# Two-model block on one core: seven-product blocks in another order, the norm scale at the residual, and a further seven-product block in quarter 0

## The chip, the cores and the metric

One NeuronCore of one Trainium2 chip runs the whole program. The metric is the device time of one execution in microseconds (us). The kernel is written against the engines directly: each engine (TensorE = PE, VectorE = DVE, ScalarE = ACT, GpSimd = POOL, SyncE = SP) has its own instruction list, and counting semaphores order them. Each engine works through its own list strictly in order.

## The reference, cut to what matters

512 tokens of width 1024 pass through a recurrent mixer, an attention mixer and then two identical hybrid layers. Only the feed-forward part at the end of each hybrid layer is touched here:

```python
def rmsnorm(x, g):
    xf = x.astype(jnp.float32)
    xf = xf * lax.rsqrt(jnp.mean(xf * xf, axis=-1, keepdims=True) + EPS)
    return (xf * g.astype(jnp.float32)).astype(x.dtype)
...
    x = x + merged @ w_o
    h2 = rmsnorm(x, norm_mlp)
    return x + jnp.square(jax.nn.relu(h2 @ w_up)) @ w_down
```

D_FF is 4096, so `w_up` is 1024 x 4096 and `w_down` 4096 x 1024. The norm's per-token factor s = 1/rms is positive, so relu(s a)^2 = s^2 relu(a)^2: the factor may be applied to the products of `w_up`, or squared and applied to the products of `w_down`.

## The kernel before

Everything is kept transposed: a tile is 128 features by 512 tokens. A **turn** (or block) gives 512 output features by 512 tokens in a set of four PSUM banks; the two sets of four banks alternate from turn to turn. Operands are split into a high and a low part of a short float format, so every product is three matmuls (high x high, low x high, high x low; L741, L742, L743). The weights come in **chunks** of 128 x 1024 numbers: SP loads a chunk into one of four `w_raw` slots, ACT rounds it into `w_hi` (L1132, `round_ahead`), and DVE subtracts to get `w_lo` (L1582, `remainder`). `w_hi` and `w_lo` have four slots as well, so a chunk can be prepared once PE has finished the chunk four places before it, and three chunks are normally ready ahead.

The feed-forward part works by **quarters** of D_FF. A quarter has two up blocks (j = 0, 1), each giving 512 features in `up_t` and then in `y_hi`/`y_lo` (relu, square, split), and two down blocks (kind `residual`, k = "y"), which multiply all 1024 features of the quarter with `w_down` and add the result to `x`. A plain block is 4 chunks of 24 matmuls over 512 tokens.

In quarters 1 to 3 both up blocks are **seven-product blocks**: a block multiplication of 2 x 2 parts that needs seven products in place of eight (`seven_products`, L753). Each product is a chunk of 24 matmuls over 256 tokens (L781, L783, L785). Four loaded weight quarters are combined on DVE (L1578, L1587, L1590, L1593, in place in `w_raw`) to four further chunks: B11, T1, T2, B21, T3, B22, T4 is the order. The combined inputs `mixed` are made once per layer in quarter 0 by the step `mix` (part 0 gives the first mixed input, part 1 the low parts of the other three). Partial sums that go to several outputs are copied by ACT, the **seeds** (L1159): after product 1 the bank `first` is copied into the bank `sum_`, after product 2 `lent` into `kept_t`, after product 3 `sum_` into `last`, after product 5 `sum_` into `kept_t`. PE's product 3 (T2) accumulates into `sum_` and so waits for the first seed.

What sets the order of work is the step list of `schedule()` and, for each step, the order in which each engine's function writes its instructions: on ACT `split_ahead` (weights and seeds of the block), then `join` (a wait for all that the engines did before), then the step's own work; on DVE the same without seeds. `led` says that a block's chunk 3 was prepared by the step before. In `up_of_seven` DVE waits for the end of the block, then reads all four banks, scales by `rms`, squares and splits, and ACT makes the high parts in between.

## Time and profile before

| what | value |
|---|---|
| median of 3 runs | 2188.85 us (2188.39 to 2189.55) |
| the profiled execution's own time | 2187.33 us |
| its span (first to last instruction) | 2185.5 us |
| PE busy | 2123.3 us, 97% of the span |
| DVE busy | 1429.0 us, 65% |
| ACT busy | 906.1 us, 41% |
| DMA | 212.02 MB, the queue that carries the weights takes 31.0% of 16 engines' time |
| mean granted PE clock | 0.988 |

The page says how much of the span each engine is busy, which wait was the longest, and how the chain of work that ended last divides: here 78% of it is PE. Matmuls overlap in the pipeline (each is shown 0.38 us long and starts 0.216 us after the one before), so their rate is read from start times.

### The profile page before, as it was taken

Reading aid. Unit: us, or ns where it says so; the run is one execution under the profiler, and the core shown is the slowest. Engines: PE = TensorE matmul, PEld = TensorE weight load, DVE = VectorE, ACT = ScalarE, POOL = GpSimd, SP = SyncE. Lnnn points to the kernel's source line nnn. Section 1 sums busy time; section 2 is a strip of 40 time slices with the busy share of each in tenths; the row PEclk is TensorE's granted clock in tenths of the full one; section 3 lists DMA queues with packets and bytes.
Section 4 is the critical chain, followed back from the end, with each engine's and each line's share of the span. In section 5 each row is a group of like instructions: output and inputs, shape, how many; then the busy total and the mean of one; then the engine's idle time right before and its main releaser. Section 6 shows DMA issues by size and latency. Waiting matters only on the chain.

```text
span 2185.5 us, 27736 instructions
## 1 busy us (share of the span) xinstructions
PE 2123.3 (97%) x11076; PEld 1871.5 (86%) x11086; DVE 1429.0 (65%) x1984; ACT 906.1 (41%) x1271; POOL 1.4 (0%) x6
## 2 busy tenths in 40 slices
PE   9989999999999999999988989999999999989888
PEld 8878878788888888888888988888888888889887
DVE  8888785768665554566677576665445656776665
ACT  6775473636344213234333244443212224342342
POOL 0000000000000000000000000000000000000000
PEclk9999999999999999999999999999999999999999
DMA  5333212223332323333231333233333333232322
GB/s 180 114 100 103 87 59 86 70 82 97 97 96 78 106 87 116 106 89 106 86 114 51 116 116 106 78 92 91 98 105 98 105 101 89 81 116 77 116 93 91
DMA packets 59535, 212.02 MB, mean 97 GB/s; under 512 B 6736, under 2 KB 7120, under 8 KB 59280
## 3 DMA queue, kind: packets, MB, share of 16 engines
q1 hardware_dynamic: 59040, 208.83, 31.0%
q8 instruction: 88, 1.44, 0.3%
q0 software_dynamic: 224, 1.31, 0.2%
q14 instruction: 39, 0.32, 0.0%
q10 hardware_dynamic: 144, 0.12, 0.0%
HBM read 208.14 MB, written 2.10 MB: 96 GB/s over the span
## 4 chain that ended last, share of the span: by engine, by line
PE 78%; DVE 8%; ACT 2%; issue 1%; DVEq 0%; ACTq 0%
PE bank L741 20%; PE bank L742 20%; PE bank L743 20%; PE bank L781 2%; PE bank L783 2%; PE bank L785 2%; PE bank L736 2%; PE bank L737 2%; PE bank L738 2%; DVE w_lo L1582 1%; PE bank L973 1%; DVE arena L2269 1%; ACT w_hi L1132 1%; PE bank L965 1%; DVE y_lo L1636 0%
## 5 line engine op out<-in xcount | busy, mean ns | idle before, releaser
L1582 DVE TENSOR_TENSOR w_lo<-w_raw,w_hi 128x1024 fp32r<-128x1024 f32 x423 | 508.4, 1214 | 580.5 <-ACT w_hi L1132 579.2
L1132 ACT ACTIVATE w_hi<-w_raw 128x1024 fp32r<-128x1024 f32 x423 | 436.6, 1046 | 727.4 <-PE bank L743 641.7
L741 PE MATMUL bank<-h_both,w_hi 128*128 128x512 f32 x1404 | 535.8, 382 | 2.1 <-DVE arena L1631 1.1
L742 PE MATMUL bank<-h_both,w_hi 128*128 128x512 f32 x1404 | 532.1, 379 | 0.0
L743 PE MATMUL bank<-h_both,w_lo 128*128 128x512 f32 x1404 | 532.1, 379 | 0.0
L741 PE MATMUL bank<-y_hi,w_hi 128*128 128x512 f32 x1048 | 399.0, 381 | 7.8 <-DVE y_lo L1636 5.8
L742 PE MATMUL bank<-y_lo,w_hi 128*128 128x512 f32 x1048 | 397.8, 380 | 0.0
L743 PE MATMUL bank<-y_hi,w_lo 128*128 128x512 f32 x1048 | 397.8, 380 | 0.0
L741 PEld LDWEIGHTS bank<-h_both,w_hi 128*128 128x128 f32 x1404 | 265.4, 189 | 42.8 <-issue 3.9
L742 PEld LDWEIGHTS bank<-h_both,w_hi 128*128 128x128 f32 x1404 | 265.4, 189 | 38.4 <-issue 1.4
L743 PEld LDWEIGHTS bank<-h_both,w_lo 128*128 128x128 f32 x1404 | 265.4, 189 | 37.8
L741 PEld LDWEIGHTS bank<-y_hi,w_hi 128*128 128x128 f32 x1048 | 198.4, 189 | 38.0 <-DVE w_lo L1582 4.5
L743 PEld LDWEIGHTS bank<-y_hi,w_lo 128*128 128x128 f32 x1048 | 198.5, 189 | 28.3
L742 PEld LDWEIGHTS bank<-y_lo,w_hi 128*128 128x128 f32 x1048 | 198.5, 189 | 28.1 <-issue 0.2
L1197 ACT ACTIVATE y_hi<-arena 128x512 fp32r<-128x512 f32 x144 | 86.9, 630 | 187.7 <-DVE arena L2269 69.8
L781 PE MATMUL bank<-mixed,w_hi 128*128 128x256 f32 x384 | 112.4, 293 | 36.9 <-DVE y_lo L1636 36.9
L781 PEld LDWEIGHTS bank<-mixed,w_hi 128*128 128x128 f32 x384 | 79.3, 206 | 37.9 <-issue 37.9
L783 PE MATMUL bank<-mixed,w_hi 128*128 128x256 f32 x384 | 111.4, 290 | 0.0
L785 PE MATMUL bank<-mixed,w_lo 128*128 128x256 f32 x384 | 111.0, 289 | 0.0
L1631 DVE TENSOR_TENSOR arena<-bank,rms 128x512 f32<-128x512 f32 x120 | 76.0, 686 | 22.8 <-PE bank L743 21.7
L1636 DVE TENSOR_TENSOR y_lo<-arena,y_hi 128x512 fp32r<-128x512 f32 x128 | 79.7, 683 | 0.2 <-ACT y_hi L1197 0.2
L781 PE MATMUL bank<-h_both,w_hi 128*128 128x256 f32 x288 | 79.6, 276 | 0.0
(271 smaller groups left out, 2492.9 us busy)
## 6 DMA issues: line engine op xcount, KB each, us to landing
w_raw<-in_stream SPq DMA_DIRECT2D x389, 512.0 KB, 3.7
x<-in_x_t SPq DMA_DIRECT2D x8, 256.0 KB, 6.9
out_t<-x SPq DMA_DIRECT2D x8, 256.0 KB, 2.1
arena<-in_consts POOLq DMA_DIRECT2D x1, 1024.0 KB, 5.3
w_raw<-in_stream SPq DMA_DIRECT2D x2, 256.0 KB, 4.3
arena<-in_positions POOLq DMA_DIRECT2D x1, 256.0 KB, 6.0
vec_t<-in_vecs ACTq DMA_DIRECT2D x1, 112.5 KB, 3.3
ident<-in_consts SPq DMA_DIRECT2D x1, 64.0 KB, 6.9
```

Source lines behind the costliest of these rows:

```text
L736: pe.matmul(out, a_h[:, t], w_h, start=first, stop=False)
L741: pe.matmul(out, w_hi[:, slot, w], streamed(a_h), start=first, stop=False)
L742: pe.matmul(out, w_hi[:, slot, w], streamed(a_l), start=False, stop=False)
L743: mm = pe.matmul(out, w_lo[:, slot, w], streamed(a_h), start=False, stop=last)
L781: pe.matmul(out, w_hi[:, slot, w], tokens(tile(0, k)), start=begin, stop=False, skip_group_check=True)
L783: pe.matmul(out, w_hi[:, slot, w], tokens(tile(1, k)), start=False, stop=False, skip_group_check=True)
L785: mm = pe.matmul(out, w_lo[:, slot, w], tokens(tile(0, k)), start=False, stop=end, skip_group_check=True)
L1132: A.activation(w_hi[:, slot, w], w_raw[:, chunks.raw_slot[raw], w], ACT.Copy).then_inc(hi_ready, 1)
L1197: A.activation(y_hi[:, slot, :], src, ACT.Copy).then_inc(a_hi, 1)
L1582: V.tensor_tensor(w_lo[:, slot, w], src[:, w], w_hi[:, slot, w].bitcast(F32), ALU.subtract).then_inc(lo_ready, 1)
L1631: V.tensor_tensor(halves(tile(n)), product_bank(n), halves(rms[:, :]), ALU.mult).then_inc(evacuated, 1)
L1636: V.tensor_tensor(y_lo[:, slot(n), :], tile(n), y_hi[:, slot(n), :].bitcast(F32), ALU.subtract).then_inc(a_lo, 1)
```

## The change

1. `first_up` runs `mix` part 0, up block j = 0 (plain), `mix` part 1, and then up block j = 1 as a seven-product block. Before it ran up 0, `mix` 0, up 1, `mix` 1, with both blocks plain.
2. The norm's factor is no longer applied to the up products. The statistics are taken in quarter 0's first down block, ACT writes the mean of squares without the root (Identity in place of Sqrt), and DVE multiplies each down product by its reciprocal before it is added to `x` (`scaled_residual`): two DVE operations per bank in place of one.
3. Seven-product blocks have an order of their own on ACT and DVE (`seven`). ACT reads `first` after product 4 and `sum_` after the block's end (Relu), squares two tiles, and the squares and high parts of these two tiles (`left_over`) are moved behind the first seed of the next block if that is a seven-product block too. DVE reads only `last` and the kept tiles, and multiplies with relu in one operation.
4. The plain up block has relu, square and high part on ACT, and only the low part on DVE.
5. The tiles of `y` are made and used in the order 2, 3, 0, 1 (`PART_ORDER`), and the rows of `w_down` are laid out to suit.

```diff
     "merge": {"vec": 4, **SPLIT},
-    "up": {"vec": 4, **SPLIT},
+    "up": {"act_out": 4, **SPLIT},
...
-        return [s("up", 4, 1, True, j=0), s("mix", part=0), s("up", 4, 1, j=1, led=True), s("mix", part=1)]
-
-    def down():
-        return [s("residual", 4, 1, k="y", j=0), s("residual", 4, 1, k="y", j=1)]
+        return [s("mix", part=0), s("up", 4, 1, j=0, led=True), s("mix", part=1), s("up", 0, 1, j=1, seven=True)]
+
+    def down(stats=False):
+        return [s("residual", 4, 1, stats, k="y", j=0, scaled=True), s("residual", 4, 1, k="y", j=1, scaled=True)]
```

On ACT, the new function `seven`:

```diff
+                if not step.args.get("led"):
+                    act.wait_ge(bank_ready, before)
+                    ahead(3)
+                products(1)
+                keep(sum_, first)
+                run_left_over()
+                ahead(4)
+                products(2)
+                keep(kept(T, 0), lent)
+                ahead(5)
+                products(3)
+                keep(last, sum_)
+                ahead(6)
+                products(4)
+
+                act.wait_ge(a_lo, T.value("a_lo"))
+                act.wait_ge(evacuated, before)
+                positive(first, slice(0, SEQ // 2)).then_inc(evacuated, 1)
+                ahead(7)
+                products(5)
+                keep(kept(T, 1), sum_)
+                ahead(8)
+                products(6)
+                ahead(9)
+                for n in (2, 3):
+                    act.wait_ge(vec, T.value("vec", n + 1))
+                    hi(n, up_t[:, n, :], slot + n)
+                act.wait_ge(bank_ready, done)
+                positive(sum_, slice(SEQ // 2, SEQ)).then_inc(evacuated, 3)
+                ahead(10)
...
+                left_over.append(rest)
+                if not step.args["paired"]:
+                    run_left_over()
...
-                A.activation(rms[:, :], bank[set_ + 3][:, :], ACT.Sqrt, scale=1.0 / D,
+                squared = step.kind == "residual"
+                A.activation(rms[:, :], bank[set_ + 3][:, :], ACT.Identity if squared else ACT.Sqrt, scale=1.0 / D,
```

On DVE, in `scaled_residual` (the order of a down block is scale 0, scale 1, add 0, scale 2, add 1, scale 3, add 2, add 3; at the program's last block it is scale and add, bank by bank):

```diff
+                def scale(n):
+                    nonlocal counted
+                    banks(n)
+                    V.tensor_tensor(halves(up_t[:, n, :]), product_bank(n), halves(rms[:, :]), ALU.mult).then_inc(vec, 1)
...
+                def add(n):
+                    got(scaled_at[n])
+                    x_n = x[:, 4 * j + n, :]
+                    V.tensor_tensor(x_n, up_t[:, n, :], x_n, ALU.add).then_inc(evacuated, 1)
```

And on DVE, its `seven`:

```diff
+                ahead(4)
+                run_left_over()
+                for n in range(5, 9):
+                    ahead(n)
...
+                V.tensor_tensor(up_pair(2, slice(SEQ // 2, SEQ)), kept_sum, kept_lent, ALU.add).then_inc(vec, 1)
+                ahead(9)
+                dve.wait_ge(chunk_used, T.value("used", 6))
+                V.tensor_tensor(up_pair(2, slice(0, SEQ // 2)), last, kept_lent, ALU.add).then_inc(vec, 1)
+                got(2)
+                for n in range(2, 4):
                     V.scalar_tensor_tensor(out=up_t[:, n, :], in0=up_t[:, n, :], scalar=0.0, in1=up_t[:, n, :],
                                            op0=ALU.max, op1=ALU.mult).then_inc(vec, 1)
+                low(2, 1)
+                low(3, 2)
+                ahead(10)
```

**Place one: ACT, from the end of a pair's first seven-product block into its second (quarters 1 to 3).** `w_hi` is a chunk's high part, `y_hi<-arena` the high part of an up tile, `bank<-bank` the first seed, on which product 3 of the second block waits. Before:

```order
L1132 ACTIVATE w_hi<-w_raw 128x1024 x3
L1197 ACTIVATE y_hi<-arena 128x512 x4
L1159 ACTIVATE bank<-bank 128x512
L1132 ACTIVATE w_hi<-w_raw 128x1024
L1159 ACTIVATE kept_t<-bank 128x512
```

Now:

```order
L1192 ACTIVATE arena<-bank 128x2x256
L1154 ACTIVATE w_hi<-w_raw 128x1024
L1189 ACTIVATE kept_t<-bank 128x512
L1154 ACTIVATE w_hi<-w_raw 128x1024 x2
L1274 ACTIVATE y_hi<-arena 128x512 x2
L1192 ACTIVATE arena<-bank 128x2x256
L1154 ACTIVATE w_hi<-w_raw 128x1024
L1189 ACTIVATE bank<-bank 128x512
L1229 ACTIVATE arena<-arena 128x512 x2
L1274 ACTIVATE y_hi<-arena 128x512 x2
L1154 ACTIVATE w_hi<-w_raw 128x1024
```

Four high parts stood ahead of the first seed; now two high parts, a relu read of a bank and one chunk stand there, and two squares and two high parts stand behind it.

**Place two: DVE, in quarter 0, around the second mixing (before, the first mixing and up block 1 stand with it).** `arena<-x,vec_t,arena` are the mixing sums, `mixed` their low parts. Before:

```order
L1582 TENSOR_TENSOR w_lo<-w_raw,w_hi 128x1024
L2226 SCALAR_TENSOR_TENSOR arena<-x,vec_t,arena 128x256 x4
L2234 SCALAR_TENSOR_TENSOR arena<-x,vec_t,arena 128x256 x4
L2243 TENSOR_TENSOR mixed<-arena,mixed 128x1024
L1582 TENSOR_TENSOR w_lo<-w_raw,w_hi 128x1024 x3
L1631 TENSOR_TENSOR arena<-bank,rms 128x512 x4
L2294 SCALAR_TENSOR_TENSOR arena<-arena 128x512 x4
L1636 TENSOR_TENSOR y_lo<-arena,y_hi 128x512 x4
L2229 SCALAR_TENSOR_TENSOR arena<-x,vec_t,arena 128x256 x4
L2237 SCALAR_TENSOR_TENSOR arena<-x,vec_t,arena 128x256 x4
L2243 TENSOR_TENSOR mixed<-arena,mixed 128x1024 x3
L1582 TENSOR_TENSOR w_lo<-w_raw,w_hi 128x1024 x4
```

Now:

```order
L1667 TENSOR_TENSOR w_lo<-w_raw,w_hi 128x1024
L1675 TENSOR_TENSOR w_raw<-w_raw 128x1024
L1667 TENSOR_TENSOR w_lo<-w_raw,w_hi 128x1024
L2416 TENSOR_TENSOR y_lo<-arena,y_hi 128x512 x4
L2350 SCALAR_TENSOR_TENSOR arena<-x,vec_t,arena 128x256 x4
L2358 SCALAR_TENSOR_TENSOR arena<-x,vec_t,arena 128x256 x4
L2364 TENSOR_TENSOR mixed<-arena,mixed 128x1024 x3
L1667 TENSOR_TENSOR w_lo<-w_raw,w_hi 128x1024
L1678 TENSOR_TENSOR w_raw<-w_raw 128x1024
L1667 TENSOR_TENSOR w_lo<-w_raw,w_hi 128x1024 x5
```

Before, two down blocks followed the second mixing; now the seven-product block j = 1, whose product 3 reads the first of these three `mixed` low parts, is the very next block. The scale and the squares (L1631, L2294) have left DVE for ACT.

## Rows read from the trace of the kernel before

**Rows 1.** The page's busy time, share and instructions of each engine.

```profile
PE 2123.3 (97%) x11076; PEld 1871.5 (86%) x11086; DVE 1429.0 (65%) x1984; ACT 906.1 (41%) x1271; POOL 1.4 (0%) x6
```

**Rows 2.** The waits, PE's two largest: us in total, times, longest us.

```profile
PE bank L781 <- DVE y_lo L1636: 36.9, 6, 6.2
...
PE bank L741 <- DVE y_lo L1636: 5.8, 3, 3.4
```

**Rows 3.** Six stretches, one per seven-product pair: sum in us, busy times and means.

```profile
sum 276.41, PE 239.51 PEld 238.54 DVE 193.59 ACT 125.79 POOL 0.00; mean PE 39.92 PEld 39.76 DVE 32.26 ACT 20.97 POOL 0.00
```

**Rows 4.** PE in order of time: first matmuls of blocks, and after the stall.

```profile
995.57 0.38 PE L741 MATMUL bank<-h_both,w_hi 128*128 128x512 f32 x1
...
1080.78 0.27 PE L781 MATMUL bank<-h_both,w_hi 128*128 128x256 f32 x1
...
1099.53 0.28 PE L781 MATMUL bank<-h_both,w_hi 128*128 128x256 f32 x1
...
1111.21 0.55 PE L781 MATMUL bank<-mixed,w_hi 128*128 128x256 f32 x1 [6.15 <-DVE y_lo L1636]
...
1126.76 0.38 PE L741 MATMUL bank<-y_hi,w_hi 128*128 128x512 f32 x1
...
1168.20 0.27 PE L781 MATMUL bank<-h_both,w_hi 128*128 128x256 f32 x1
```

**Rows 5.** ACT in order of time, before the second block's first seed.

```profile
1109.34 1.23 ACT L1197 ACTIVATE y_hi<-arena 128x512 fp32r<-128x512 f32 x2 [1.23 <-DVE arena L2269]
1110.48 0.58 ACT L1159 ACTIVATE bank<-bank 128x512 f32<-128x512 f32 x1
```

**Rows 6.** Stretches with a PE pause: the third figure from the end is the granted clock.

```profile
1104.98:1111.20 6.22, 0.08 (x1) 0.03 (x1) 6.19 (x10) 3.09 (x6) 0.00 (x0) 0.80 0.00 0
1111.20:1116.04 4.84, 4.83 (x25) 4.84 (x26) 3.48 (x4) 2.26 (x3) 0.00 (x0) 0.55 0.30 78
284.00:290.00 6.00, 4.27 (x20) 3.44 (x19) 5.84 (x9) 2.72 (x4) 0.00 (x0) 1.00 0.07 10
```

**Rows 7.** PE in quarter 0: the second down chunk waits for `y_lo`.

```profile
1041.82 0.48 PE L741 MATMUL bank<-y_hi,w_hi 128*128 128x512 f32 x1 [1.20 <-DVE y_lo L1636]
```

**Rows 8.** DVE and ACT in a pair's first block (it starts at 1168.20).

```profile
1166.56 2.54 DVE L1829 TENSOR_TENSOR x<-bank,x 128x512 f32<-128x512 f32 x4 [1.02 <-PE bank L743]
...
1179.12 1.06 ACT L1132 ACTIVATE w_hi<-w_raw 128x1024 fp32r<-128x1024 f32 x1 [1.14 <-PE bank L785]
...
1185.26 1.23 DVE L1590 TENSOR_TENSOR w_raw<-w_raw 128x1024 f32<-128x1024 f32 x1
```

**Rows 9.** Groups of instructions by line and shape: busy us, mean ns, idle before.

```profile
L1636 DVE TENSOR_TENSOR y_lo<-arena,y_hi 128x512 fp32r<-128x512 f32 x128 | 79.7, 683 | 0.2 <-ACT y_hi L1197 0.2
L1281 ACT ACTIVATE arena<-x 128x512 f32<-128x512 f32 x44 | 27.0, 622 | 18.1 <-DVE x L1829 12.3 <-DVE sumsq L1746 4.4 <-DVE sumsq L1743 1.0
L2263 DVE TENSOR_TENSOR arena<-bank,kept_t 128x512 f32<-128x512 f32 x12 | 9.2, 770 | 0.0
```

**Rows 10.** ACT and DVE in quarter 0: after the norm, up block 1, second mixing.

```profile
1000.94 1.99 ACT L1132 ACTIVATE w_hi<-w_raw 128x1024 fp32r<-128x1024 f32 x2
...
1036.23 2.54 DVE L1631 TENSOR_TENSOR arena<-bank,rms 128x512 f32<-128x512 f32 x4 [0.89 <-PE bank L743]
...
1041.09 2.49 DVE L1636 TENSOR_TENSOR y_lo<-arena,y_hi 128x512 fp32r<-128x512 f32 x4
1043.77 1.67 DVE L2229 SCALAR_TENSOR_TENSOR arena<-x,vec_t,arena 128x256 f32<-128x256 f32 x4 [0.20 <-issue]
...
1047.06 3.50 DVE L2243 TENSOR_TENSOR mixed<-arena,mixed 128x1024 fp32r<-128x1024 f32 x3
...
1048.03 2.94 ACT L1132 ACTIVATE w_hi<-w_raw 128x1024 fp32r<-128x1024 f32 x3
```

**Rows 11.** DVE at the end of the program.

```profile
2169.60 1.28 DVE L1829 TENSOR_TENSOR x<-bank,x 128x512 f32<-128x512 f32 x2
...
2172.87 0.68 DVE L1829 TENSOR_TENSOR x<-bank,x 128x512 f32<-128x512 f32 x1
```

More of the change, by code:

```diff
@@ L293, in schedule @@
             after.args["led"] = True
+            step.args["paired"] = bool(after.args.get("seven"))
     return items
@@ L1137, in split_ahead @@
                     part_before[0] = step.args.get("part")
-                if step.args.get("seven") and step.args.get("led"):
-                    seeds(0)
                 for n, slot in [next_slot(T)] if runs_ahead(step) else split_slots(T, step):
@@ L1147, in split_ahead, with run_left_over, seven, products @@
                     round_ahead(n, slot)
-                    if step.args.get("seven"):
-                        seeds(n - RING + 1)
-            def seeds(used):
+            left_over = []
+            def run_left_over():
+                while left_over:
+                    left_over.pop(0)()
+            def seven(step):
+                part_before[0] = None
                 set_ = 4 * (T.fixed["turn"] % 2)
                 first, lent, sum_, last = (bank[set_ + n][:, :] for n in range(4))
-                for at, out, src in ((1, sum_, first), (2, kept(T, 0), lent), (3, last, sum_), (5, kept(T, 1), sum_)):
-                    if at == used + 1:
-                        act.wait_ge(chunk_used, T.value("used", at))
-                        A.activation(out, src, ACT.Copy).then_inc(seeded, 1)
+                slot = 4 * step.args["j"]
+                before, done = T.value("turn", 0, 4), T.value("turn", 4, 4)
+                def products(n):
+                    act.wait_ge(chunk_used, T.value("used", n))
+                def ahead(n):
+                    round_ahead(n, (T.fixed["chunk"] + n) % RING)
+                def keep(out, src):
+                    A.activation(out, src, ACT.Copy).then_inc(seeded, 1)
+                def positive(src, t):
+                    return A.activation(up_pair(0, t), bank_pair(src), ACT.Relu)
+                if not step.args.get("led"):
[27 more added lines that the diff above has]
+                ahead(10)
+                outs = T.value("act_out")
+                def rest():
+                    for n in range(2):
+                        act.wait_ge(evacuated, done)
+                        A.activation(up_t[:, n, :], up_t[:, n, :], ACT.Square).then_inc(act_out, 1)
+                    for n in range(2):
+                        act.wait_ge(act_out, outs + n + 1)
+                        hi(n, up_t[:, n, :], slot + n)
+                left_over.append(rest)
+                if not step.args["paired"]:
+                    run_left_over()
@@ new lines, in _, with run_left_over, seven, ahead @@
+            left_over = []
+            def run_left_over():
+                while left_over:
+                    left_over.pop(0)()
+            def seven(step):
+                last = bank_pair(the_bank(3)[:, :])
+                kept_lent, kept_sum = (bank_pair(kept(T, n)) for n in range(2))
+                slot, highs = 4 * step.args["j"], T.value("a_hi")
+                def ahead(n):
+                    remainder(n, (T.fixed["chunk"] + n) % RING)
+                def low(n, count):
+                    dve.wait_ge(a_hi, highs + count)
+                    V.tensor_tensor(y_lo[:, slot + n, :], up_t[:, n, :], y_hi[:, slot + n, :].bitcast(F32),
+                                    ALU.subtract).then_inc(a_lo, 1)
+                if not step.args.get("led"):
+                    ahead(3)
+                ahead(4)
+                run_left_over()
+                for n in range(5, 9):
+                    ahead(n)
+                dve.wait_ge(a_lo, T.value("a_lo"))
+                dve.wait_ge(evacuated, T.value("turn", 0, 4))
+                dve.wait_ge(seeded, T.value("seeds", 4))
+                V.tensor_tensor(up_pair(2, slice(SEQ // 2, SEQ)), kept_sum, kept_lent, ALU.add).then_inc(vec, 1)
[4 more added lines that the diff above has]
+                for n in range(2, 4):
@@ L2309, in emit @@
             def emit(step):
+                if step.args.get("seven"):
+                    seven(step)
+                    return
                 closing = step.args.get("part") == "close" and step.kind in ("x", "lru_gate", "residual")
@@ L2370, in order_of_weights @@
             q = args["quarter"]
-            out.append(group(w_down[layer], [(512 * j, 512)], slice(1024 * q, 1024 * q + 1024)))
+            rows = np.concatenate([np.arange(P) + 1024 * q + P * k for k in Y_ORDER])
+            out.append(group(w_down[layer], [(512 * j, 512)], rows))
         elif kind == "forget":
```

123 lines of the change are left out of this document (69 added, 54 removed).

## Prediction, made before the changed kernel had run

> **What bounds the kernel now.** The page comes first: PE is busy for 2123.3 of 2185.5 us [rows 1], so only two things can pay: less matmul work, and the some 62 us in which PE waits. The view of waits says where they are: 36.9 us in six pauses at L781, the longest 6.2, and 5.8 us at L741 [rows 2]. The stretches then give the price of the six. A pair of seven-product blocks should take two blocks' work. The first block of the pair at 1080.78 lasts 18.75 us, to 1099.53 [rows 4]; its second, to 1126.76, lasts 27.23. The six pairs took 276.41 us [rows 3] where 12 x 18.76 = 225.1 is work, so the pauses cost **51.3 us**, 8.55 each, and not 6.15. The rest is the clock: it was granted at 0.80 on average over the pause and at 0.55 in the 4.84 us after it [rows 6], so most of the product behind the pause ran at the lower level, 1.2 GHz.
>
> Who is late? PE's product 3 adds into a bank that ACT seeds, and that seed (L1159) starts at 1110.48, ends at 1111.06, and PE starts at 1111.21 [rows 4, 5]. DVE's `y_lo`, which the view names, merely ended near that time. The seed's source was ready long before; ACT stood in its list at the previous block's high parts, which wait for DVE's squares [rows 5]. An earlier seed is therefore worth the whole 51.3.
>
> **The change, part by part.** *The pairs lose the old pause*: -51.3. *Two blocks (one per layer) have seven products in place of eight*: a plain block takes (1168.20 - 1126.76)/2 = 20.72 us [rows 4], a seven-product block 18.75, so 2 x 1.97 = -3.9. *Quarter 0's down block waited for `y_lo`*: the pause shown is 1.20, and 1.36 from start to start (a matmul is drawn 0.38 long at a rate of 0.216); block j = 1 is now finished tile by tile as in the other quarters, so 2 x 1.36 = -2.7 [rows 7].
>
> *New wait in the pairs.* I count from the first block's start (1168.20 in rows 8). The second block starts at 18.75, and its product 3 is due two products of 2.68 later, at 24.1. ACT used to round chunk 7 at 10.92; now the relu read of `first` stands ahead, a bank read of 0.58 that holds ACT for about 0.55 [rows 5]. DVE's chain of splits and combinations, which waits for this chunk and ended at 1186.49, i.e. at 18.3 [rows 8], ends at 18.85. Behind it, in each engine's order: ACT rounds T2, to 20.0 (1.06); DVE splits it, to 21.2 (1.23); it adds the bank `last`, to 21.9 (0.77 [rows 9], with the usual overlap of 0.1); two squares, to 23.2; ACT makes the second high part, to 23.9; relu read of `sum_`, to 24.4; ACT rounds chunk 10, to 25.35; only then the seed, to 25.85; PE starts 0.15 later, at **26.0**. That is 1.9 late, six times: **+11.4**. The wait DVE has from doubled work at the down block (eight operations at 0.6 from -1.64 on, to 3.25 where it was 0.9 [rows 8]) is covered: chunk 3 is split by 4.4 and needed at 8.0. In the second block the seed for product 5 is done some 0.1 ahead of its use, so a little more may be lost there. The lower bound of the new wait is nothing (a chain of twelve steps has to be 1.9 shorter), the upper 3.5 (each step 0.13 longer).
>
> Does such a pause lower the clock? The gaps of 1.7 us near 287 show none: granted 1.00 [rows 6]. The pause of 6.15 does. 1.9 is much nearer to 1.7 than to 6.15, so I take no clock loss; the price of one, 2.25 a pair, stays in the range.
>
> *New wait in quarter 0.* The new seven-product block follows up block 0 at once, and its product 3 needs the second mixing and a seed. Count from up block 0's start at 995.57 [rows 4]. It ends at 20.7, and product 3 is due at 20.7 + 5.4 = 26.1. Ahead of the relus stand the first mixing and three chunks with their combinations. From the norm's end on ACT, 5.4 in (1000.94 [rows 10]): chunk 3 and four small copies until the first sum at 7.7; eight sums, 3.3 [rows 10]; a high part, 1.06; chunk 4, 0.95; its split and two combinations, 3.85; T1's split and the third combination, 2.4; T2's rounding, 1.1 [rows 8]. ACT comes to the relus at 20.35, where the banks would allow 19.1 (1.64 ahead of the block's end, as in rows 8). Four relus, four squares and four high parts on ACT at 0.6 each, then the last low part 0.7 behind: 28.3. From there the mixing is as in the trace: the sums begin 0.2 later, and ACT takes its next chunk 4.26 after them (1048.03 - 1043.77 [rows 10]), at 32.75. Chunk 3 (0.95) and the seed (0.58 + 0.15) follow: PE starts product 3 at **34.4**, 8.3 us late. The pause is longer than 6.15, so the clock falls; the six show 8.55 - 6.31 = 2.25 for it (6.31 is 6.15 plus that 0.16). Two layers: 2 x 10.6 = **+21.2**. A check from the old run: bank read to the last low part took 1036.23 to 1043.58, and the mixing followed it; that chain was hidden behind two down blocks, and this cover is gone.
>
> *The end.* DVE's last adds ran from 2169.60 to 2173.55 [rows 11] with six operations; there are ten now, at 0.6, and four of them wait for the one before (0.1 each): the end is at 2176.1, **+2.5**, nothing beside it. *Hidden*: the reciprocal and Identity read in the down block (the table load of Sqrt goes), the down blocks' second operation elsewhere (DVE is at 65% [rows 1]), and the DMAs: a seven-product block loads four chunks as a plain one does. At the layer's end, the norm's high and low parts come up to 2.4 later, but their first use is two chunks into the next block.
>
> **Sum.** -51.3 - 3.9 - 2.7 + 11.4 + 21.2 + 2.5 = -22.8 against the profiled execution's 2187.33: 2164.5. The median of the runs is 1.5 above that execution, so **2166.0**.
>
> **Rivals.**
> - *Pairs without a wait.* The chain has twelve steps and is 1.9 too long; if banks are read faster and steps overlap more, it closes: 2166 - 11.4 = 2154.6. For it: DVE is free 1.2 us in the chain before. Against: every duration is from a row.
> - *The clock falls in the pairs too.* If 1.9 us is enough, each pair pays 2.25 more: 2166 + 13.5 = 2179.5. Against it are the gaps near 287. The Trainium skill (TensorE: Matmul & The Clock Gate, A second HAM failure mode) reports a clock that swings from short pauses between groups of matmuls; no row here shows that.
> - *Quarter 0 is covered.* If the second mixing isn't waited for as I read it, 21.2 goes: 2144.8. Against: place two of the order has nothing between the mixing and the block.
> - *Slower: relu on ACT.* No row shows a Relu on ACT, and it now stands twice on each pair's chain and four times in quarter 0's. Were it three times the 0.62 of a plain ACT operation [rows 9], each pair would wait 2.4 more and also lose the clock (6 x 4.65 = 27.9), quarter 0 4.8 more per layer (9.6): 2203.5. It decides from about 1.5 us per relu. Against: ACT's squares of this shape take 0.62 where DVE takes 0.68 [rows 9]. The Trainium skill (ScalarE: Activation LUTs, Rules for kernel authors) wants relu on VectorE, up to about 3 times faster in bf16; here all is f32, and the rows show no such lead.
> - *The change doesn't do what it says*, the early seed not being reached because ACT waits for `y_lo` ahead of it: the order shows it ahead of the left-over work, so this has no more than its part of the last 2%.
>
> **How the numbers follow.** Forecast 0.62, pairs closed 0.12, clock in the pairs 0.12, quarter 0 covered 0.08, slower by relu 0.04, something between 0.02. The predicted time is the forecast's. That case's own range: the pairs' wait 0.9 to 2.9 (6 us either way) and quarter 0's 1.5 us per layer either way give 2157 to 2175. With most of the closed pairs and of the clock case the range is 2153 to 2178; left out are quarter 0 covered, the slow case and the edges. A measurement tells some 0.2% (4.4 us) from no change. All cases but the slow one are faster by more: faster 0.95, same 0.015, slower 0.035.
>
> **What would show it.** A PE pause of about 1.9 us at product 3 of each pair's second block, ended by ACT's seed, with the clock at 1.00; a pause of about 8 us at product 3 in quarter 0 of each layer, and a lower clock behind it; pairs of 39.4 us; no pause at the down blocks; the last `x` add some 3.6 us after PE's last product. The prediction is wrong if the pairs' pauses exceed 3 us or are missing, if quarter 0's pause is under 6, or if a Relu on ACT takes over 0.8 us.

## The result, and the profile after

| | before | changed |
|---|---|---|
| median of the runs, us | 2188.70 (2188.39 to 2189.55) | 2165.13 (2163.96 to 2165.24) |
| span of the profiled execution, us | 2185.5 | 2163.3 |
| ratio of the times | 1 | 0.989, 95% interval 0.9873 to 0.9908 |

The change is worth 23.6 us, 1.1%; the interval of the ratio leaves out 1, and the prediction took 4.4 us (0.2%) as the least that can be told from no change. The two spans differ by 22.2 us. First the page's busy time of each engine, after the change:

```profile
PE 2113.3 (98%) x11230; PEld 1866.1 (86%) x11230; DVE 1427.8 (66%) x1978; ACT 947.8 (44%) x1357; POOL 1.4 (0%) x6
```

PE has 10 us less drawn work than in [rows 1] (some of that is the clock: a matmul at the lower level is drawn longer) and 12 us less idle time. ACT has 42 us more and remains under half. What PE waits for has changed its name. The view of waits, its two largest (us in total, times, longest us):

```profile
PE bank L793 <- ACT bank L1189: 24.9, 8, 7.7
PE bank L750 <- DVE y_lo L1721: 3.4, 1, 3.4
```

In [rows 2] the same place of the program had six pauses of 6.15; now there are eight, ended by ACT's seed (L1189). Two of them, 7.65 each, are new and stand in quarter 0 of each layer; the other six are the pairs', 1.60 each. The 5.8 us of the second line in [rows 2] were two waits of 1.20 at the down blocks and one of 3.4 near the program's start; only the 3.4 is left. The six stretches of the pairs, the first and the sum (us, busy time of PE, PEld, DVE, ACT, POOL with their counts, granted clock, DMA share, GB/s):

```profile
1087.83:1127.19 39.36, 37.76 (x338) 37.59 (x337) 31.85 (x35) 23.11 (x31) 0.00 (x0) 1.00 0.37 122
...
sum 236.12, PE 226.52 PEld 225.54 DVE 189.96 ACT 138.59 POOL 0.00; mean PE 37.75 PEld 37.59 DVE 31.66 ACT 23.10 POOL 0.00
```

Against [rows 3] the pairs take 236.12 where they took 276.41: 40.3 us less. 225.1 of it is work, so 11.0 us, 1.84 a pair, are still lost. The clock was granted in full in all six. Now one pair in order of time, PE and then ACT and DVE (start, duration, engine, line, operation, in brackets the idle time before it and what ended it):

```profile
1168.63 0.27 PE L793 MATMUL bank<-h_both,w_hi 128*128 128x256 f32 x1
...
1194.51 0.35 PE L793 MATMUL bank<-mixed,w_hi 128*128 128x256 f32 x1 [1.60 <-ACT bank L1189]
```

```profile
1179.55 0.60 ACT L1192 ACTIVATE arena<-bank 128x512 f32<-128x512 f32 x1 [1.14 <-PE bank L797]
1180.04 1.05 ACT L1154 ACTIVATE w_hi<-w_raw 128x1024 fp32r<-128x1024 f32 x1
...
1187.49 1.06 ACT L1154 ACTIVATE w_hi<-w_raw 128x1024 fp32r<-128x1024 f32 x1 [2.72 <-DVE w_raw L1675]
1191.21 1.23 ACT L1274 ACTIVATE y_hi<-arena 128x512 fp32r<-128x512 f32 x2 [2.67 <-DVE arena L2401]
1192.35 0.58 ACT L1192 ACTIVATE arena<-bank 128x512 f32<-128x512 f32 x1
1192.83 1.05 ACT L1154 ACTIVATE w_hi<-w_raw 128x1024 fp32r<-128x1024 f32 x1
1193.78 0.59 ACT L1189 ACTIVATE bank<-bank 128x512 f32<-128x512 f32 x1
```

```profile
1186.17 1.22 DVE L1675 TENSOR_TENSOR w_raw<-w_raw 128x1024 f32<-128x1024 f32 x1
...
1188.58 1.22 DVE L1667 TENSOR_TENSOR w_lo<-w_raw,w_hi 128x1024 fp32r<-128x1024 f32 x1 [0.49 <-ACT w_hi L1154]
1189.73 0.73 DVE L2398 TENSOR_TENSOR arena<-bank,kept_t 128x512 f32<-128x512 f32 x1
1190.49 1.29 DVE L2401 SCALAR_TENSOR_TENSOR arena<-arena 128x512 f32<-128x512 f32 x2
```

This is the chain of twelve steps. Read it from the back: the seed at 1193.78 waits in ACT's list behind a slice's high part, a relu and the two high parts; these wait for DVE's two squares; DVE comes to the squares behind the last slices' splits. No step of it idles except at a hand-over between the two engines.

Quarter 0 of layer 0, ACT and PE:

```profile
1016.32 2.04 ACT L1593 ACTIVATE arena<-bank 128x512 f32<-128x512 f32 x4
1018.23 2.21 ACT L1596 ACTIVATE arena<-arena 128x512 f32<-128x512 f32 x4
1020.31 2.20 ACT L1274 ACTIVATE y_hi<-arena 128x512 fp32r<-128x512 f32 x4
...
1028.03 1.04 ACT L1154 ACTIVATE w_hi<-w_raw 128x1024 fp32r<-128x1024 f32 x1
1028.97 0.58 ACT L1189 ACTIVATE bank<-bank 128x512 f32<-128x512 f32 x1
```

```profile
1016.52 0.27 PE L793 MATMUL bank<-h_both,w_hi 128*128 128x256 f32 x1
...
1029.69 0.55 PE L793 MATMUL bank<-mixed,w_hi 128*128 128x256 f32 x1 [7.65 <-ACT bank L1189]
```

```profile
1027.06 3.50 DVE L2364 TENSOR_TENSOR mixed<-arena,mixed 128x1024 fp32r<-128x1024 f32 x3
```

The seven-product block starts at 1016.52. Its product 3 was due two products of 2.68 later, at 1021.88, and came 7.81 late; product 4 was due at 1024.56 and came at 1034.81, 10.25 late. The 2.44 between them are the clock (below).

The view names the seed, which ended at 1029.55, as what ended the pause. A second thing was late with it: product 3 also reads the first of the three low parts of the second mixing (the DVE row), which took 1.22 and ended at 1028.3. With the seed out of the way product 3 could have started some 0.15 later, at about 1028.4, an estimate from the usual hand-over: still 6.5 of the 7.8 us late. So here it is the whole second mixing that is late, and the seed behind it adds 1.3.

The stretches of the pause and of the product behind it (the third figure from the end is the granted clock; in the pairs above it was 1.00):

```profile
1022.04:1029.69 7.65, 0.00 (x1) 0.03 (x1) 7.43 (x14) 4.16 (x6) 0.00 (x0) 0.66 0.00 0
1029.69:1034.81 5.12, 5.12 (x24) 5.12 (x25) 5.12 (x5) 2.26 (x3) 0.00 (x0) 0.52 0.01 3
```

Last, the tail. From the start of the last product's last matmul to the end of the span the kernel before takes 2185.5 - 2172.13 = 13.4 us, the changed one 2163.3 - 2145.75 = 17.55. First the changed kernel's rows, then those of before:

```profile
2145.75 0.38 PE L821 MATMUL bank<-y_hi,w_lo 128*128 128x512 f32 x1
...
2149.12 0.69 DVE L1934 TENSOR_TENSOR x<-arena,x 128x512 f32<-128x512 f32 x1
...
2152.26 1.28 ACT L1494 ACT_TABLE_LOAD   x1 [1.79 <-PE bank L1080]
```

```profile
2172.13 0.38 PE L809 MATMUL bank<-y_hi,w_lo 128*128 128x512 f32 x1
...
2176.09 0.26 ACT L1417 ACTIVATE rms_col<-bank,eps_t 128x4 f32<-128x4 f32 x1 [1.88 <-PE bank L1066]
```

The last `x` add ends 1.42 us behind that matmul's start in the kernel before (2173.55 from [rows 11]) and 4.06 behind it in the changed one (2149.81): +2.6. A table load of 1.28 us has appeared between the last sums and the root: +1.3.

So the time went this way: pairs -40.3; quarter 0, from its first up block to the first pair, 92.03 us (995.80 to 1087.83) where it was 85.21 (995.57 to 1080.78 in [rows 4]), +6.8 a layer, +13.6; the tail +4.2. That is -22.5, and the spans say -22.2.

### The profile page after: what moved, and what is told of

Its sections match the earlier page's. It is cut to its first block and busy times, and to the rows that moved or that the text cites. A ratio compares the mean times of both kernels' runs of the same rounds, so it can differ in the third digit from the quotient of the medians.

```text
span 2163.3 us, 28022 instructions
## 1 busy us (share of the span) xinstructions
PE 2113.3 (98%) x11230; PEld 1866.1 (86%) x11230; DVE 1427.8 (66%) x1978; ACT 947.8 (44%) x1357; POOL 1.4 (0%) x6
## 5 line engine op out<-in xcount | busy, mean ns | idle before, releaser
L1154 ACT ACTIVATE w_hi<-w_raw 128x1024 fp32r<-128x1024 f32 x429 | 444.3, 1046 | 724.2 <-PE bank L752 641.5
L750 PE MATMUL bank<-h_both,w_hi 128*128 128x512 f32 x1340 | 510.7, 381 | 1.7 <-DVE arena L1716 1.1
L751 PE MATMUL bank<-h_both,w_hi 128*128 128x512 f32 x1340 | 507.9, 379 | 0.0
L752 PE MATMUL bank<-h_both,w_lo 128*128 128x512 f32 x1340 | 507.9, 379 | 0.0
L750 PEld LDWEIGHTS bank<-h_both,w_hi 128*128 128x128 f32 x1340 | 253.3, 189 | 40.3 <-issue 3.4
L751 PEld LDWEIGHTS bank<-h_both,w_hi 128*128 128x128 f32 x1340 | 253.3, 189 | 36.2 <-issue 1.0
L752 PEld LDWEIGHTS bank<-h_both,w_lo 128*128 128x128 f32 x1340 | 253.3, 189 | 35.9
L793 PE MATMUL bank<-mixed,w_hi 128*128 128x256 f32 x448 | 126.2, 282 | 24.9 <-ACT bank L1189 24.9
L795 PE MATMUL bank<-mixed,w_hi 128*128 128x256 f32 x448 | 125.4, 280 | 0.0
L797 PE MATMUL bank<-mixed,w_lo 128*128 128x256 f32 x448 | 125.2, 280 | 0.0
L793 PEld LDWEIGHTS bank<-mixed,w_hi 128*128 128x128 f32 x448 | 88.1, 197 | 26.2 <-issue 26.2
L795 PE MATMUL bank<-h_both,w_hi 128*128 128x256 f32 x336 | 92.4, 275 | 0.0
L797 PE MATMUL bank<-h_both,w_lo 128*128 128x256 f32 x336 | 92.4, 275 | 0.0
L793 PE MATMUL bank<-h_both,w_hi 128*128 128x256 f32 x336 | 92.4, 275 | 0.0
```

The costliest lines, as they stand in the source:

```text
L750: pe.matmul(out, w_hi[:, slot, w], streamed(a_h), start=first, stop=False)
L751: pe.matmul(out, w_hi[:, slot, w], streamed(a_l), start=False, stop=False)
L752: mm = pe.matmul(out, w_lo[:, slot, w], streamed(a_h), start=False, stop=last)
L793: pe.matmul(out, w_hi[:, slot, w], tokens(tile(0, k)), start=begin, stop=False, skip_group_check=True)
L795: pe.matmul(out, w_hi[:, slot, w], tokens(tile(1, k)), start=False, stop=False, skip_group_check=True)
L797: mm = pe.matmul(out, w_lo[:, slot, w], tokens(tile(0, k)), start=False, stop=end, skip_group_check=True)
```

## The experiments

My theory was the chain above: each late product is late through one named copy in ACT's list, a copy that isn't late by its data; take it out of the queue and the next late thing shows. It holds in the changed kernel's pairs; in quarter 0 (above) and in the kernel before (below) something else was late together with the copy. The rivals are put beside it in each expectation. Line numbers differ a little between the kernels; the operations are the same.

### Is the first seed worth 51.3 us in the kernel before?

```
 # kernel before, ACT, up block of seven products, behind the last slice's rounding
+if step.args["j"] == 0:
+    other = 4 - 4 * (T.fixed["turn"] % 2)
+    act.wait_ge(evacuated, T.value("turn", 0, 4))
+    act.wait_ge(chunk_used, T.value("used", 7))
+    A.activation(bank[other + 2][:, :], bank[other][:, :], ACT.Copy).then_inc(seeded, 1)
 split_vec(...)          # four high parts
 # and the second block leaves out its own first seed
```

> The kernel before with one edit: ACT issues the second seven block's first seed (the copy from the block's first bank to its third) ahead of the first block's four high parts, not behind them; the norm scale stays in the up blocks, the order of the parts stays. Theory (the late thing is then the next one, because VectorE still does the scale, the squared relu and four low parts of the first block before it reaches the second block's fifth slice): product 3 starts on time, product 5 then waits some 3.5 us for its low part, and with the clock that falls each of the six pairs still loses 5 to 6 us of the 8.55 it lost; some 18 us are gained, about 2171 us. Rival (what the prediction says in a sentence: an earlier seed is worth the whole 51.3 us): no pause is left in the pairs, about 2137 us.

Measured: 2169.97 us (2166.74 to 2170.63), ratio 0.991 [0.9894, 0.9927]. The waits, a pair's pause, and what DVE and ACT did just before its end:

```profile
PE bank L781 <- DVE w_lo L1593: 19.0, 6, 3.2
...
1113.89 0.35 PE L781 MATMUL bank<-mixed,w_hi 128*128 128x256 f32 x1 [3.18 <-DVE w_lo L1593]
...
1112.53 3.49 DVE L1593 TENSOR_TENSOR w_lo<-w_raw,w_hi 128x1024 fp32r<-128x1024 f32 x3
...
1113.15 0.59 ACT L1165 ACTIVATE bank<-bank 128x512 f32<-128x512 f32 x1
```

The pause at product 3 is gone and another of 3.18 has come at product 5. The view says that DVE ended it. But product 5 needs two things, its slice's low part (the first of DVE's three, ended at 1113.75) and the third seed (ACT's copy, ended at 1113.74), and in all six pairs the two end within 0.02 us of each other. In DVE's list the low part stood behind the previous block's scale, squares and low parts; in ACT's list the seed stood behind the previous block's high parts, which wait for DVE's squares. The six pairs took 258.68 us, 5.6 lost in each. So an earlier seed alone is worth 18.9 us in this kernel (2188.91 in the runs beside it; 17.7 of it in the pairs), not 51.3. What is left stands on both engines behind the first block's work on DVE. The changed kernel makes that work less (the scale is out of the up block) and moves some of it behind the next block's first slices (the leftover); no run here separates the two.

### What does quarter 0 cost?

```
-return [s("mix", part=0), s("up", 4, 1, j=0, led=True), s("mix", part=1), s("up", 0, 1, j=1, seven=True)]
+return [s("up", 4, 1, j=0), s("mix", part=0), s("up", 4, 1, j=1, led=True), s("mix", part=1)]
```

> The changed kernel with quarter 0's two up blocks both plain and in the order that they had before (up, mix, up, mix), all else as changed. Theory (the second block's late first seed costs its pause and the clock's fall, 10.25 us a layer as the trace of the changed kernel has it): 2165.1 - 20.5, + 3.9 for the two blocks' eighth products, + 2.7 if the wait for the low part at the down block comes back: 2148.5 to 2151.3 us. Rival (the pause is paid elsewhere: TensorE waits for something else of quarter 0 when the seed is out of the way, or the clock falls there whatever the order): 2158 us or more.

Measured: 2153.67 us (2152.42 to 2154.81), ratio to the kernel before 0.984 [0.9825, 0.9854]. This part of the change, taken by itself, loses 11.5 us. The clock stays in full from the program's early part to its tail, and the wait at the down block is back:

```profile
1041.01 0.48 PE L750 MATMUL bank<-y_hi,w_hi 128*128 128x512 f32 x1 [1.51 <-DVE y_lo L2416]
...
1107.07 0.35 PE L793 MATMUL bank<-mixed,w_hi 128*128 128x256 f32 x1 [1.97 <-ACT bank L1189]
```

From its first up block at 995.30 to the first pair at 1080.82 quarter 0 takes 85.5 us where it took 92.0: 6.5 less, against 10.25 - 1.97 for an eighth product - 1.67 for the wait (1.51, and 0.16 for the way a matmul is drawn) = 6.6. Two layers give 13.0. 0.4 is lost again in the first pair (1.97 in place of 1.60), and 1.1 in the tail, where the clock falls sooner (below); that leaves 11.5. The spans differ by 12.1, of which 0.5 lies ahead of quarter 0. The median is 2.4 above the band's upper edge for these reasons; the rival (2158 or more) is out.

### Where is a pair's 1.60 us?

Three runs take the chain apart. The first moves the seed alone. In ACT's list it goes ahead of the two high parts and also of the relu of `sum_` and of chunk 10's high part behind them.

```
 ahead(9)
+if step.args["paired"]:
+    products(7)
+    keep(bank[4 - set_ + 2][:, :], bank[4 - set_][:, :])
 for n in (2, 3):
 # and the second block leaves out its own first seed
```

> The changed kernel with the paired second block's first seed moved ahead of the first block's high parts of rows 2 and 3 on ACT. Theory (each pair loses 1.6 us at product 3 and 0.25 behind it; with product 3 on time the next late thing is product 5, whose slice's split stands behind the same work): product 3 starts on time, product 5 pauses 0.5 to 1 us, the six pairs gain 0.9 to 1.3 us each: 2157.5 to 2160 us. Rival A: all of 11 us, 2154 us, and no pause in the pairs. Rival B (ACT's high parts of rows 2 and 3, now later, hold up VectorE's low parts and what is queued behind them): no gain, 2165 us.

Measured: 2159.98 us (2159.58 to 2160.53), ratio 0.9869 [0.9854, 0.9884]. Product 3 is on time, and product 5 now pauses:

```profile
1197.35 0.35 PE L793 MATMUL bank<-mixed,w_hi 128*128 128x256 f32 x1 [0.69 <-ACT bank L1189]
...
sum 230.70, PE 226.52 PEld 225.52 DVE 186.88 ACT 138.98 POOL 0.00; mean PE 37.75 PEld 37.59 DVE 31.15 ACT 23.16 POOL 0.00
```

The six pairs gained 5.4 us of their 11.0; the theory had 5 to 7.6. What is late next is a seed too, the third, and not a slice's split, as the expectation gave for the place.

The second run keeps that and moves the third seed too.

```
+if step.args.get("led"):
+    products(3)
+    keep(last, sum_)
+    ahead(5)
+else:
     ahead(5)
     products(3)
     keep(last, sum_)
```

> As seed_ahead (the paired second block's first seed ahead of the first block's high parts of rows 2 and 3), and in the second block of a pair ACT copies the third seed (from the third bank to the fourth) ahead of the fifth slice's high part, not behind it. Theory (the 0.69 us pause that seed_ahead left before product 5 is that copy, standing 0.6 us behind a high part that is not due yet): the pause is gone, or under 0.2 us, and the six pairs gain 0.7 us each over seed_ahead: 2160.0 - 4.2 = 2155.8 us. Rival (the fifth slice's high part, now later, makes VectorE's low part the late one): the pause stays at 0.5 us or more with VectorE's low part as what ended it, 2160 us.

Measured: 2157.07 us (2154.93 to 2157.39), ratio 0.9855 [0.984, 0.9869]: 2.9 us under the run before it, where 4.2 were expected. The profiled execution was the fastest of the four by 1.9 us or more; its pairs' own sum gives 4.05:

```profile
sum 226.65, PE 226.63 PEld 225.60 DVE 183.47 ACT 138.63 POOL 0.00; mean PE 37.77 PEld 37.60 DVE 30.58 ACT 23.11 POOL 0.00
```

PE is busy for 226.63 of 226.65 us. No pause is left in the pairs (the sum is 1.5 us over the 225.1 of work), and no slice's low part came late in the seeds' place.

The third run asks where the chain begins.

```
-positive(first, slice(0, SEQ // 2)).then_inc(evacuated, 1)
 ahead(7)
+positive(first, slice(0, SEQ // 2)).then_inc(evacuated, 1)
```

> The changed kernel with two ACT steps of every seven block exchanged: the high part of slice 7 (the next block's first but two) is made ahead of the relu of the block's first bank, not behind it. Slice 7 waits for a transfer and its use comes later than the relu could start. Theory (the first seed of a pair's second block is late by the sum of what ACT has queued ahead of it since the last product of the first block, which begins with the relus; what stands between them before that is free): the pause at product 3 stays at 1.60 us to within 0.1. Rival (the whole queue of ACT is late already by slice 7, so an exchange there moves the chain): the pause changes by 0.5 us or more, either way. Span 2163.3 us by the theory, and 2160 or 2167 us by the rival.

Measured, in one execution: 2161.01 us, span 2159.2, against 2163.3. ACT and PE around the exchange (this pair starts at 1168.12):

```profile
1179.04 1.06 ACT L1154 ACTIVATE w_hi<-w_raw 128x1024 fp32r<-128x1024 f32 x1 [1.14 <-PE bank L797]
1180.01 0.58 ACT L1192 ACTIVATE arena<-bank 128x512 f32<-128x512 f32 x1
...
1193.52 0.35 PE L793 MATMUL bank<-mixed,w_hi 128*128 128x256 f32 x1 [1.12 <-ACT bank L1189]
```

Here the theory fell. The slice's high part starts 10.92 us behind the pair's start, not 11.41, and the pause 25 us later is 1.12, not 1.60: the 0.49 that the relu had held ACT went through the whole chain to the end. The six pauses were 1.12 to 1.15. The sum of the pairs is 233.34, 0.46 less for each and 2.8 in all, just under the 0.5 a pause that the rival had named. The span fell by 4.1. 1.2 of the rest is quarter 0, whose two layers took 91.9 and 91.0 us and not 92.0 and 92.1: the pause was 7.65 as before, and the granted clock 0.94 and 0.96 where it was 0.94 in both. The prediction's own step (the relu "holds ACT for about 0.55", and the chain ends that much later) was right; my doubt of it after the fact was wrong.

### Can quarter 0 keep its seven products?

```
 # ACT, quarter 0's first up block: only the four relus at its place
+if step.args.get("rest_later"):
+    return
 # squares and high parts (and DVE's low parts) as left-over work, run behind the next block's first seed
+left_over.append(rest)
```

> The changed kernel, in quarter 0 alone: ACT does only the four relus of the first up block at its place, and leaves the block's four squares and four high parts (with VectorE's four low parts) over until the seven block behind it has had its first seed. Theory (the 7.65 us pause at product 3 is the first seed standing behind the mixing's and the first block's squares and high parts): the pause falls to 2 to 3 us at product 3 with at most 1 to 2 us more behind it, the clock stays at full speed or nearly so, 12 to 14 us are gained over both layers: 2151 to 2153 us. Rival (the work left over is late for the down block, or the mixing's high parts alone hold the seed as long): a pause of 5 us or more stays in each layer, at product 3 or at the down block's start, 2157 us or more.

Measured: 2154.83 us (2153.78 to 2155.47), ratio 0.9845 [0.9829, 0.9861]. Product 3's pause and its end:

```profile
1024.20 0.55 PE L797 MATMUL bank<-mixed,w_hi 128*128 128x256 f32 x1 [2.73 <-ACT bank L1193]
```

7.65 has become 2.73, in both layers; layer 1 has one more pause of 1.45 at product 5. So the theory holds for the size of the pauses. Its cause has to be put more widely, though: not only the seed came sooner. DVE's mixing sums start 23.05 us behind the up block's start (1018.28 of 995.23), not 27.97, and those 4.92 us are what the pause lost. The first low part of the mixing ends at 1022.8 and the seed at 1024.05, so the mixing still holds product 3 by itself for 1.6 us and the seed for 1.3 more. The run moved ACT's eight operations and DVE's four low parts together and does not say which of them held the mixing. The clock was at its lower level for 3.41 us from 1024.13 on in layer 0, and stayed in full in layer 1, behind the same pause of 2.73. 10.3 us are gained where 12 to 14 were expected, a miss; 1.8 of what is missing is in the tail (below).

### The tail's 4.15 us

```
 # ACT, the last down block's squares
+A.activation(small[:, 79:80], eps_t[:, :], ACT.Sqrt)
 for i in range(DT // 2):
```

> The changed kernel with one tiny Sqrt on ACT at the start of the last down block's squares, into a cell that nothing reads afterwards, so that the function table that the final norm needs is loaded while TensorE still multiplies. Theory: the 1.28 us table load that stands between the last sums and the root in the changed kernel is gone from there, the end comes 1.2 to 1.4 us sooner after the last product (16.2 us, not 17.55), span about 2162.0 us. Rival: the load comes back before the root (a Square or a Copy in between takes the table away again): 17.5 us, span 2163.3 us.

Measured, in one execution: 2163.61 us, span 2161.7. The load now runs beside PE's products, and the root has none before it:

```profile
2141.89 1.28 ACT L1514 ACT_TABLE_LOAD   x1
2143.18 0.20 ACT L1514 ACTIVATE small<-eps_t 128x1 f32<-128x1 f32 x1
...
2151.94 0.26 ACT L1494 ACTIVATE rms_col<-bank,eps_t 128x4 f32<-128x4 f32 x1 [1.64 <-PE bank L1080]
```

The squares in between did not take the table away. The last matmul started at 2145.57, so the tail is 16.1 us, 1.4 less: the table's 1.28 and a little of the clock.

```
 # DVE, the last down block: products are added without the norm's factor
-scale(n)
-add(n)
+banks(n)
+x_n = halves(x[:, 4 * j + n, :])
+V.tensor_tensor(x_n, product_bank(n), x_n, ALU.add).then_inc(evacuated, 1)
```

> The changed kernel with the norm scale left out of the very last down block (the second down block of layer 1's last quarter adds its products to the residual without the factor): 4 of VectorE's 10 instructions after the last up block are gone, the table load stays. From the last product to the end the changed kernel takes 17.55 us and the kernel before 13.4. Theory (the 4.15 us between them are 1.3 of the table load and the rest VectorE's scales and the clock that falls sooner because of them): 14.5 to 15.0 us, span about 2160.6 us. Rival (the scales are covered by the products, the rest of the difference is the clock alone): 16.5 us or more, 2162.3 us or more.

Measured, in one execution: 2160.72 us, span 2158.8. DVE's last adds are back to six operations, and the last ends 1.42 behind the last matmul's start at 2143.81, just as in the kernel before:

```profile
2144.55 0.68 DVE L1954 TENSOR_TENSOR x<-bank,x 128x512 f32<-128x512 f32 x1
...
2147.75 1.28 ACT L1494 ACT_TABLE_LOAD   x1 [1.86 <-PE bank L1080]
```

The tail is 15.0 us: 2.55 less than 17.55. With the table's 1.4 that makes 3.95 of the 4.15.

### The edits together

Two runs join the edits. Both have the seed and the third seed ahead, slice 7 ahead of the relu, and the early Sqrt; they differ in quarter 0.

> Four of the edits together on the changed kernel: in the pairs the second block's first seed ahead of the first block's high parts, the third seed ahead of the fifth slice's high part, and slice 7's high part ahead of the first relu; quarter 0's up blocks both plain in their old order; the tiny Sqrt that loads the table early in the tail. If the places are apart (seed_and_third against the changed kernel 8.1 us, q0_plain 11.5, tail_table 1.4 to 1.6, slice 7's part nothing more because no pause is left for it in the pairs): 2165.1 - 8.1 - 11.5 - 1.5 = 2144.0 us, with 2142 to 2146 for the tail's clock. Rival (one limit stands behind two of them, so the gains overlap, for instance the first pair of a layer, which paused 1.97 us in q0_plain and not 1.60): 2148 us or more.

> The same, with quarter 0 as in q0_deferred (the first up block's squares, high and low parts left over behind the seven block's first seed), not plain. Sum: 2165.1 - 8.1 - 10.3 - 1.5 = 2145.2 us, with 2143 to 2147 for the tail's clock. Against joined_q0_plain that is 1 us slower by the sum; the rival (in quarter 0 slice 7's part ahead of the relu brings the leftover forward too, and its pause of 2.7 us falls) has it 1 us or more faster, below 2143 us.

Measured: 2143.16 us (2142.42 to 2144.93) and 2143.52 (2142.61 to 2146.47), both with the ratio 0.979 [0.9777, 0.9803] to the kernel before, whose median was 2189.46 beside them. That is 22 us (1.0%) better than the changed kernel and 46 better than before. The gains add up to within a microsecond (2144.0 expected), so the places are apart, and which order quarter 0 has can't be told apart by these runs; the plain one is the simpler. What PE waits for in the first of them:

```profile
PE bank L750 <- DVE y_lo L2426: 3.0, 2, 1.5
...
PE bank L793 <- ACT kept_t L1189: 0.8, 2, 0.5
...
1194.09 1.06 ACT L1154 ACTIVATE w_hi<-w_raw 128x1024 fp32r<-128x1024 f32 x1 [2.60 <-DMA w_raw<-in_stream]
```

The seeds' 24.9 us are down to 0.8, and nothing large is left in the up blocks. The 0.8 are the fourth seed's, the copy behind product 5 for which product 7 waits. The last row shows why: ACT waits 2.60 us for the transfer of slice 7, makes its high part, then the relu, then this seed, and product 7 pauses for 0.48 us in this pair. Without the exchange (as in the trace of `seed_and_third`) the relu is done before that wait. With the first seed moved the exchange has no pause to shorten (the pairs' sum is 227.5 here and 226.65 without it). I didn't run the joined kernel without it. In the deferred one the pause of 2.7 stayed, so its rival is out.

## Why the prediction was right, step by step

The forecast was 2166.0, the result 2165.13. That could be chance in a sum of six terms, so each is compared with its own place.

- **The pairs.** Old pauses -51.3 and a new wait of +11.4 were forecast, -39.9 together; the sums of the stretches give -40.3. The pause was to be 1.9 late with the clock in full; PE came to product 3 at 25.88 us of the pair where 24.12 was due, 1.76 late, with the clock at 1.00. The steps of the count also fit one by one: DVE's chain ended at 18.76 (18.85 forecast), ACT's rounding of T2 at 19.9 (20.0), the squares at 23.15 (23.2), the seed at 25.74 (25.85). The run with slice 7 ahead of the relu shows that the count was a chain and not a coincidence.
- **Quarter 0.** The relus start 20.5 us behind the up block's start (20.35 forecast), ACT's next slice at 32.2 (32.75), PE's product 3 at 33.9 (34.4): 7.8 late where 8.3 was forecast, and 2.4 for the clock where 2.25 was carried over from the pairs. A layer cost 10.25, not 10.6. The closeness of the clock's part is in part luck: with the same code and the same pause quarter 0 took from 91.1 to 92.3 us a layer in five kernels (the section on the hardware). With 2.0 for the eighth product and 1.4 for the wait that went, that makes 6.9, and the trace has 6.8.
- **The seven-product block in quarter 0 and the down block's wait** (-3.9, -2.7) are in that 6.8, and came back when the block was made plain again.
- **The tail** is the term that was mis-sized: +2.5 forecast, +4.2 measured. DVE's part of it was right (the last add is 2.6 later behind the product). What failed is the clause "the table load of Sqrt goes". It doesn't go: the up blocks' Sqrt had loaded the table that the final root uses, and with Identity in its place the load moves to the first Sqrt behind it, which is the root in the tail, where nothing hides it. The two tail runs put 1.4 on it and 2.55 on the scales.
- **A sentence that was wrong though no number hung on it:** "An earlier seed is therefore worth the whole 51.3." It names the last thing to arrive. In the kernel before, with that seed early, the pairs keep 33.6 of the 51.3 us, because a slice's low part and the third seed are both 3.2 us late two products on. The sum survived since its new wait was counted through the changed lists of both engines, not taken from that sentence. Likewise "the seed for product 5 is done some 0.1 ahead of its use" was right only while product 3 was late; with product 3 on time it was 0.69 late.
- **The rivals.** The clock did not fall in the pairs, quarter 0 was not covered, and a Relu on ACT took 0.60 us from a bank (2.04 for four in a row), the same as the copies beside it. The Trainium skill's wish for relu on VectorE (ScalarE: Activation LUTs, Rules for kernel authors) is for bf16. No relu alone ran on DVE here. Of f32 operations of that shape that read a bank, DVE's copy (L2076) takes 0.68 and ACT's relu 0.60, so ACT was no slower at this place. Where the source is not a bank and there is only one, DVE does have a lead in f32, in a row of the kernel before that the prediction had not read: ACT's operations take 0.62 in [rows 9], and this one on DVE 0.48:

```profile
L1942 DVE TENSOR_SCALAR arena<-arena,small 128x512 f32<-128x512 f32 x16 | 7.7, 480 | 0.0
```

Measured less forecast is -0.4 in the pairs, -1.0 in quarter 0 (13.6 against 21.2 - 3.9 - 2.7 = 14.6) and +1.7 in the tail: they partly cancelled, but none is over 2 us. On the profiled executions the forecast was 2164.5 and the result 2165.19, 0.7 over. The median came out under the forecast only because 1.5 us had been added for the distance between a profiled execution and the median, which was -0.06 this time.

## What to carry to other kernels

The wait that a profile names is the last arrival; what removing it is worth is the distance to the next one, and that has to be counted through the lists of every engine that feeds the place (here 18.9 us of 51.3). List all that a waiting product needs, with the time at which each ends: in the kernel before the next two things ended within 0.02 us of each other. Ask of a late seed or copy whether its data or its place in its engine's list holds it: two such copies, moved ahead of four operations and of one that were not urgent, gave 8 us. The quarter-0 block that was to save an eighth of its products lost more than five times that, most of it because the mixing that feeds it had no block left to hide behind. When a function disappears from ACT, ask which later call had lived on its table, and whether something still hides the load there.

## What the runs showed of the hardware

A function table's load falls to the first call that needs the table. The groups of table loads at the norm's read of the sums and at the root, first of the kernel before, then of the changed one (the other loads are the same in both):

```profile
L1193 ACT ACT_TABLE_LOAD x3 | 3.8, 1283 | 0.1
```

```profile
L1270 ACT ACT_TABLE_LOAD x2 | 2.6, 1283 | 0.0
...
L1494 ACT ACT_TABLE_LOAD x1 | 1.3, 1283 | 1.8 <-PE bank L1080 1.8
```

As many loads as before, but one of them has gone from a covered place to one with nothing beside it. A Sqrt of one column, 0.20 us, moved it back beside the products, and the Squares between it and the root left the table in place. The Trainium skill (ScalarE activation tables: per-element evaluation and per-set limits, What a function is on this engine) gives a load as 1283 ns, and the trace agrees: 1.28.

The length of a pause does not settle by itself what the clock does. Pauses of 1.60 in the pairs left it at 1.00; one of 2.73 in quarter 0 was followed by 3.41 us at the lower level in layer 0 and by none in layer 1. The 7.65 us pause stands in five kernels with the same quarter-0 code (the changed one, `seed_ahead`, `seed_and_third`, `tail_table`, `tail_unscaled`), and from its first up block to the first pair quarter 0 took between 91.1 us (layer 1 of `seed_and_third`, granted clock 0.96) and 92.3 (layer 0 of `tail_table`, 0.94). The tail shows the same: its code is equal in the changed kernel, in `q0_plain` and in `q0_deferred`, but the clock fell 5.06, 3.71 and 2.64 us behind the last product, and the tails took 17.55, 18.65 and 19.37 us. The stretches of the last:

```profile
2134.23:2136.87 2.64, 0.38 (x2) 0.00 (x0) 2.60 (x5) 1.10 (x2) 0.00 (x0) 1.00 0.00 0
2136.87:2153.60 16.73, 6.37 (x28) 5.91 (x28) 6.92 (x12) 2.33 (x4) 0.00 (x0) 0.50 0.34 125
```

So a microsecond or two of the difference between two of these kernels can come from where in the tail the clock falls, which is why the joined sums carry a band of 2 us. What sets that moment is open; no run here was made for it.
